# Host-laid inputs and a split first slab, and a last norm finished with tokens on partitions

## What is computed

```python
def rms_norm(x, gain):
    xf = x.astype(jnp.float32)
    y = xf * lax.rsqrt(jnp.mean(xf * xf, axis=-1, keepdims=True) + NORM_EPS)
    return (y * gain.astype(jnp.float32)).astype(x.dtype)
...
h = rms_norm(x, norm_mix[i])
q, kc, vc, ks, vs, kw, vw, gt = jnp.split(h @ w_in, splits, axis=-1)
```

## Time and profile before

| | us |
|---|---|
| median of 3 runs | 1273.48 |
| lowest, highest | 1270.31, 1273.67 |
| profiled execution | 1273.24 |
| its span in the trace | 1271.4 |
| TensorE busy (matmuls) | 1195.2 (94%) |
| DVE, ACT, POOL busy | 765.0, 565.6, 452.6 |

### The profile page before, as it was taken

One profiled execution on the slowest core, in us unless ns is written; L12 is line 12 of the kernel. 1 busy time (PEld: TensorE's weight loads), 2 busy tenths in 40 slices (PEclk: granted clock), 3 DMA queues, 4 the chain that ended last, 5 costly groups with the idle time before them and its releaser, 6 DMA issues.

```text
span 1271.4 us, 23862 instructions
## 1 busy us (share of the span) xinstructions
PE 1195.2 (94%) x9313; PEld 1130.8 (89%) x9313; DVE 765.0 (60%) x1093; ACT 565.6 (44%) x788; POOL 452.6 (36%) x430
## 2 busy tenths in 40 slices
PE   6998999999999888999999999998988898999996
PEld 5987678999999875999999998988978896999996
DVE  5753564767655566676765464436755657777544
ACT  4232344554544444455454336644353444545432
POOL 4522232266630433166651211113431303666401
PEclk9998799999999989999999999998999999999998
DMA  6651001666645540466665453243341453667551
GB/s 200 205 192 41 9 26 34 200 176 188 188 160 183 164 134 2 120 178 187 177 197 182 149 173 127 69 129 104 101 133 34 148 165 87 191 174 196 180 169 50
DMA packets 224581, 175.49 MB, mean 138 GB/s; under 512 B 7796, under 2 KB 205788, under 8 KB 224380
## 3 DMA queue, kind: packets, MB, share of 16 engines
q1 hardware_dynamic: 219052, 168.33, 44.4%
q10 hardware_dynamic: 5424, 6.09, 1.4%
...
HBM read 173.39 MB, written 1.05 MB: 137 GB/s over the span
## 4 chain that ended last, share of the span: by engine, by line
PE 81%; DVE 8%; ACT 3%; issue 3%; POOL 3%; DMA 1%; SPq 0%; ACTq 0%; DVEq 0%; POOLq 0%
PE bank L574 22%; PE bank L580 22%; PE bank L575 21%; PE bank L840 2%; DVE w_l L1512 2%; ACT w_h L1157 2%; PE bank L608 2%; PE bank L614 1%; PE bank L704 1%; PE bank L1013 1%; PE bank L808 1%; POOL work L2261 1%; DVE work L1627 1%; PE bank L848 1%; PE bank L692 1%
## 5 line engine op out<-in xcount | busy, mean ns | idle before, releaser
L574 PE MATMUL bank<-xh,w_h 128*128 128x256 f32 (+2 forms) x1792 | 451.6, 289 | 5.5 <-DVE xl L1530 4.1
L575 PE MATMUL bank<-xl,w_h 128*128 128x256 f32 (+2 forms) x1792 | 443.0, 284 | 0.0
L574 PEld LDWEIGHTS bank<-xh,w_h 128*128 128x128 f32 x1792 | 339.9, 190 | 8.5 <-issue 5.1
L575 PEld LDWEIGHTS bank<-xl,w_h 128*128 128x128 f32 x1792 | 340.8, 190 | 1.0
L1512 DVE TENSOR_TENSOR w_l<-raw,w_h 128x2048 fp32r<-128x2048 f32 (+3 forms) x95 | 212.2, 2234 | 158.6 <-ACT w_h L1157 158.5
L1157 ACT ACTIVATE w_h<-raw 128x2048 fp32r<-128x2048 f32 (+3 forms) x95 | 173.3, 1825 | 241.7 <-PE bank L580 220.5
L580 PE MATMUL bank<-xh,w_l 128*128 128x256 f32 (+2 forms) x1792 | 251.4, 283 | 2.9 <-DVE w_l L1512 2.9
L580 PEld LDWEIGHTS bank<-xh,w_l 128*128 128x128 f32 x1792 | 230.5, 189 | 3.3 <-DVE w_l L1512 3.1
L2183 POOL TENSOR_TENSOR work<-work 128x256 f32<-128x256 f32 x66 | 162.9, 2469 | 140.4 <-ACT work L1300 140.4
L1795 DVE TENSOR_TENSOR w_l<-raw,w_h 128x2048 fp32r<-128x2048 f32 x66 | 151.4, 2293 | 14.0 <-ACT w_h L1296 13.8
L574 PE MATMUL bank<-hid_h,w_h 128*128 128x256 f32 (+1 forms) x592 | 148.0, 284 | 2.5 <-issue 1.8
...
## 6 DMA issues: line engine op xcount, KB each, us to landing
...
raw<-in_w_in SPq DMA_DIRECT2D x26, 1024.0 KB, 5.2
...
raw<-in_nsa_w_in SPq DMA_DIRECT2D x10, 1024.0 KB, 5.4
...
raw<-in_swa_w_qkv SPq DMA_DIRECT2D x5, 1024.0 KB, 5.3
```

The costliest lines, as they stand in the source:

```text
L574: mm(dst, parts[0][:, k, cols], high, start=first, stop=False)
L575: mm(dst, parts[0][:, k, cols], low, start=False, stop=False)
```

## The change

**The host** lays out `x` with features on partitions (`xt_c`), the gains and biases as one table (`gain_c`), the convolution taps, position table and meta tokens likewise (`packed`). **The opening:** SP loads `x` in four parts and slab 0 in two halves, in the order part, half, part, part, half, part; the constants move behind slab 1 on the same queue, and three packed loads replace the 23. The transposes of `x` and of the small vectors are gone. `first_opening` computes chunks 0 and 1 together, half a slab at a time. ACT and DVE split slab 0 by halves. The table of roots is loaded first on ACT; `ones` is filled by POOL. **The end:** TensorE turns `h2` to tokens-on-partitions before the last FFN (`h_turn`, copied by ACT's `take_h` to `h_tok`). DVE's take of a last chunk also multiplies by the gain, ACT squares straight from the bank; `token_squares` sums them per token, with tokens on partitions, into two columns; `y_turn` turns the scaled chunks; then the root and reciprocal are of [128, 2], and the output is `bank * rstd + h_tok` in four pieces, three by DVE and one by ACT and POOL, with an output DMA for each.

```diff

     gains = [A["norm_mix"][0], A["norm_ffn"][0], A["norm_mix"][1], A["norm_ffn"][1], A["norm_final"],
...
+    xt = np.asarray(A["x"])[0].T.reshape(KC, 128, T1).transpose(1, 0, 2).reshape(128, KC * T1)
+    meta = np.asarray(A["meta_tokens_2"]).T.reshape(KC, 128, META).transpose(1, 0, 2)
+    return {"xt_c": xt, "gain_c": tab[:, 0], "taps_c": tab[:, 1:4], "pe_c": np.concatenate([pe, pe], 0), "meta_c": meta}


...
+        h_tok = work[:, stage + 3 * GN * T2:stage + 3 * GN * T2 + 2048].rearrange("p (b n) -> p b n", b=2)
+        o_sb = big[:, 0:2048].rearrange("p (b n) -> p b n", b=2)
+        y_part = big[:, 2048:2560]
+        tok_root, tok_rstd = meta_rstd[:, 0:2], meta_rstd[:, 2:4]
...
+        PIECES = [(0, 0, (y_taken, 1)), (1, 0, (y_stored, 2)), (0, 1, (y_taken, 2)), (1, 1, (y_taken, 3))]
+        Y_BANK = {(0, 0): 0, (1, 0): 1, (0, 1): 2, (1, 1): 4}
+        H_BANK = {(0, 0): 4, (1, 0): 5, (0, 1): 6, (1, 1): 3}
...
-            for tb in range(2):
-                sp.dma_start(x_in[:, tb, :], A["x"][0][128 * tb:128 * tb + 128, :]).then_inc(x_loaded, 16)
-            issue(0)
+            def x_part(j):
+                sp.dma_start(xT[:, 2 * j:2 * j + 2, 0:T1], A["xt_c"][:, 512 * j:512 * j + 512]
+                             .rearrange("p (c t) -> p c t", c=2)).then_inc(x_loaded[j], 16)
+
+            (whole, source), = slabs[0]
+            for half in range(2):
+                ks = slice(4 * half, 4 * half + 4)
+                x_part(2 * half)
+                sp.dma_start(whole[:, ks, :], source[:, ks, :]).then_inc(first_loaded[half], 16)
+                x_part(2 * half + 1)
             issue(1)
-            sp.wait_ge(prepared, 1)
-            for dst, src in vec_loads:
-                sp.dma_start(dst, src).then_inc(vec_loaded, 16)
+            sp.dma_start(early[:, :], A["early_c"]).then_inc(early_loaded, 16)
+            sp.dma_start(h2[:, :, 0:META], A["meta_c"]).then_inc(vec_loaded, 16)
+            sp.dma_start(pe_dup, A["pe_c"]).then_inc(vec_loaded, 16)
+            sp.dma_start(vecs[:, 1:4, :], A["taps_c"]).then_inc(vec_loaded, 16)
...
+            for k, (tb, half, by) in enumerate(PIECES):
+                sp.wait_ge(*by)
+                cols = slice(512 * half, 512 * half + 512)
+                sp.dma_start(out[0][128 * tb:128 * tb + 128, cols], o_sb[:, tb, cols]).then_inc(out_stored, 16)
...
-            pe.wait_ge(early_loaded, 16)
-            pe.wait_ge(x_loaded, 32)
-            for b in range(4):
-                turn([(bank[b][:, 256 * c + 128 * tb:256 * c + 128 * tb + 128],
-                          x_in[:, tb, 128 * (2 * b + c):128 * (2 * b + c) + 128]) for c in range(2) for tb in range(2)],
-                     turn_done)
-            pe.wait_ge(gain_loaded, 16)
-            turn([(bank[4][:, 0:KC], vec_in[0:KC, 0, :])], turn_done)
-
-            def turn_small():
-
-                pe.wait_ge(vec_loaded, 16 * len(vec_loads))
-                turn([(bank[5][:, 128 * v:128 * v + 128], vec_in[:, v, :]) for v in range(4)], turn_done)
...
+            def first_opening():
+
+                parts = view(w_h, 0, KC, 256), view(w_l, 0, KC, 256)
+                for half in range(2):
+                    ks = range(4 * half, 4 * half + 4)
+                    if half:
+                        pe.wait_ge(w_hi, 1)
+                    else:
+                        pe.wait_ge(first_hi, 1)
+                    for k in ks:
+                        pe.wait_ge(xl_ready, k + 1)
+                        for c in range(2):
+                            high_terms(bank[c][:, 0:T1], parts, k, slice(128 * c, 128 * c + 128), xh[:, k, 0:T1], xl[:, k, 0:T1],
+                                       k == 0)
+                    if half:
+                        pe.wait_ge(w_lo, 1)
+                    else:
+                        pe.wait_ge(first_lo, 1)
+                    for c in range(2):
+                        last = low_terms(bank[c][:, 0:T1], parts, [(k, k) for k in ks], slice(128 * c, 128 * c + 128),
+                                         xh[:, :, 0:T1], half == 1)
+                        if half:
+                            last.then_inc(proj_done, 1)
+                line["n"] += 2
...
+            first_opening()
+            pe.wait_ge(prepared, 1)
+            sum_squares(0, T1, 0, 8)
+            pe.wait_ge(early_loaded, 16)
+            m = 1
+            for n in range(2, 21):
                 if n <= 12 and n % 2 == 0 or n > 12 and n % 2:
...
+                if n in (2, 3):
+                    permute((proj_taken, n - 1))
...
+            def token_squares(c0, c1):
+
+                for c in range(c0, c1):
+                    pe.wait_ge(sq_ready, SQ_AT[8] + c + 1)
+                    for tb in range(2):
+                        last = mm(bank[7][:, tb:tb + 1], sq[:, c % 4, 128 * tb:128 * tb + 128], ones[:, 0:1], start=c == 0 and tb == 0, stop=c == 7,
+                                  skip_group_check=True)
+                    last.then_inc(ss_step, 1)
+
+            def y_turn(half):
+
+                for tb in range(2):
+                    turn([(bank[Y_BANK[tb, half]][:, 128 * c:128 * c + 128], xT[:, 4 * half + c, 128 * tb:128 * tb + 128])
+                          for c in range(4)], y_turned)
+
+            def h_turn(c):
+
+                for tb in range(2):
+                    last = nc.tensor.transpose(bank[H_BANK[tb, c // 4]][:, 128 * (c % 4):128 * (c % 4) + 128],
+                                               h2[:, c, META + 128 * tb:META + 128 * tb + 128], ident)
+                    if c % 4 == 3:
+                        last.then_inc(h_turned, 1)
+
...
+                if l == 2:
+                    pe.wait_ge(h_tok_ready, 4)
...
+                            if part == 0 and g and c == 3 and l == 2:
+                                pe.wait_ge(sq_ready, SQ_AT[8] + 4)
...
-                            sum_squares(norm, T, 0, 4)
+                            token_squares(0, 4)
+                            y_turn(0)
...
-                    sum_squares(norm, T, 4, 8)
+                    token_squares(4, 8)
+                    y_turn(1)
...
-            sum_squares(7, T2, 0, 8, LEAD)
+            for c in range(8):
+                sum_squares(7, T2, c, c + 1, LEAD)
+                if c == 4:
+                    pe.wait_ge(proj_taken, N_FFN[2])
+                h_turn(c)
...
-            act.dma_start(early[:, :], A["early_c"]).then_inc(early_loaded, 16)
+            act.dma_start(vecs[:, 0, :], A["gain_c"]).then_inc(gain_loaded, 16)
             act.wait_ge(prepared, 1)
-            act.dma_start(*gain_load).then_inc(gain_loaded, 16)
-            high(0)
+            fn(scrap[:, :], eps_col[:, 0:1], ACT.Sqrt)
...
+            act.wait_ge(gain_loaded, 16)
+            for half in range(2):
+                at = slice(1024 * half, 1024 * half + 1024)
+                for c in (4 * half + 1, 4 * half + 3):
+                    act.wait_ge(x_loaded[c // 2], 16)
+                    line.put(fn(xh[:, c, 0:T1], xT[:, c, 0:T1], ACT.Copy, scale=vec("g", c)), xh_odd)
+                    if c % 4 == 1:
+                        act.wait_ge(first_loaded[half], 16)
+                        fn(w_h[:, 0, at], raw[:, 0, at], ACT.Copy).then_inc(w_hi if half else first_hi, 1)
+            squares(0, T1, xT, lambda c: (x_loaded[c // 2], 16), lambda c: high(1) if c == 3 else None)
...
+            def down_last():
+
+                l, m = 2, ffn_at[2][1] + FC
+                for x in range(2, 8):
+                    high(m + x)
+                for c in range(8):
+                    if c == 4:
+                        preload_root()
+                    act.wait_ge(proj_taken, N_FFN[l] + 44 + c + 1)
+                    if c >= 4:
+                        act.wait_ge(ss_step, SS_AT[8] + c - 3)
+                    line.put(fn(sq[:, c % 4, 0:T1], bank[bank_of(N_FFN[l] + 44 + c)][:, 0:T1], ACT.Square), sq_ready)
+                    if c == 3:
+                        for x in range(8, 12):
+                            high(m + x)
+                act.wait_ge(ss_step, SS_AT[8] + 8)
+                line.put(fn(tok_root, bank[7][:, 0:2], ACT.Sqrt, bias=eps_col[:, 0:1]), root_ready)
+                tb, half, _ = PIECES[1]
+                act.wait_ge(y_scaled, 1)
+                act.wait_ge(y_turned, 1 + tb + 2 * half)
+                line.put(fn(y_part, bank[Y_BANK[tb, half]][:, :], ACT.Copy, scale=tok_rstd[:, tb:tb + 1]), y_stored)
+
+            def take_h():
+
+                for k, (tb, half) in enumerate(((0, 0), (1, 0), (0, 1), (1, 1))):
+                    act.wait_ge(h_turned, k + 1)
+                    line.put(fn(h_tok[:, tb, 512 * half:512 * half + 512], bank[H_BANK[tb, half]][:, :], ACT.Copy), h_tok_ready)
...
+            def first_low(half):
+
+                at = slice(1024 * half, 1024 * half + 1024)
+                if half:
+                    dve.wait_ge(w_hi, 1)
+                else:
+                    dve.wait_ge(first_hi, 1)
```

(41 more changed lines are left out.)

152 lines of the change are left out of this document (44 added, 108 removed).

## The result

The changed kernel took 1251.7 us, the median of four runs from 1249.96 to 1253.73, against 1271.89 for four runs of the kernel before beside it: a ratio of 0.9846, 95% interval 0.9813 to 0.9880, which is 1.5% less time. Its profiled execution took 1250.05 us (span 1248.3), the one before 1273.24 (span 1271.4). The forecast was 1255.0 with a range of 1250 to 1262. Later, with more runs, the change had a median of 1253.55 (six runs) against 1272.36 (eleven).

What follows compares the result with a forecast made beforehand. TensorE was taken to bound the kernel, with 81% of the chain, work being worth removing only where it waits. The terms -10.3 + 0.3 + 0.5 - 8.7 = -18.2 from the median 1273.48 gave 1255.0 us, range 1250 to 1262.

Steps and rivals of the forecast that it cites:

- Opening, 10.3: Start of kernel: chunk 2 starts at 18.2 instead of 28.58, gaining 10.3 us; bounds 7.9 and about 11.3.
- paced by ACT: Opening's sums of squares: squares 5 to 8 wait for four slots, so the old 3.62 us was kept.
- Is it kept: Chunk 4: opening's gain survives, slab 2's w_h and w_l ready with margins of 1.0 and 0.5 us.
- Entry of the last FFN, cost 0.3: Before the last FFN's first up matmul: 16 added transposes of h2 cost 0.3 us, from -0.9 to 0.7.
- wins at most 0.9: Last FFN's first 16 matmuls: 2.74 us, 1.9 at full pace, so a clock staying up wins at most 0.9.
- Down projection, cost 0.5: Last FFN's down projection: eight added transposes 0.94, sums 1.1 instead of 1.54; cost 0.5 us, bounds 0.4 and 1.3.
- The end, 8.7: After the last square: shorter root, reciprocal and output chain, span ending 1262.7 against 1271.4; gain 8.7 us, bounds 7.3 and 9.3.
- the late clock: Rival, opening: clock rises only at the old 20.0, gain there 7.9, total 1257.4 us; chance 0.12.
- POOL holds SP's queue: Rival, end: POOL's addition delays SP's queue and two pieces behind it; gain there 7.3, total 1256.4 us; chance 0.07.
- The supply: Rival, chunk 4: late tables make TensorE wait, one us per us past 22; more likely 1258 us; chance 0.10.
- the slower case: Rival, first projections: TensorE stays at 1.2 GHz, each us costing 0.5; 0.3% slower at 44 us; chance 0.01.

Runs made afterwards that it cites:

- opening_two: The change with ACT making xh of blocks 4 to 7, sums 0 to 3 earlier, all squares before slab 1's split: 1254.89 us, ratio 0.9836 to before.
- tables_late: The change with the three packed tables issued behind slabs 2 and 3: chunk 4 starts 9.03 us behind chunk 2 instead of 7.01.
- fill_alone: New opening with the old end, plus 16 unused identity transposes between the last FFN's sums of squares: first up matmul to low terms 2.0 us.
- change_repeat: The changed kernel itself, run again unaltered: median 1253.55 us of six runs; its profiled execution took 1262.25.
- both_bounds: The change with VectorE making w_l earlier, 15 extra matmuls before the first, POOL's output piece issued last: 1251.06 us, ratio 0.9833 to before.

## Why the prediction was right

*Opening, 10.3: right, 10.2 at chunk 4 and 10.0 from 60 us on, with luck in it.* First matmul 6.8, measured 6.95; end of the opening 14.6, measured 14.56; chunk 2 at 18.2, measured 17.83. Three sub-steps were off. The second half slab landed at 9.50, not 8.4; the low clock still hid it. The sums of squares took 3.27 us, not 3.62: that row counts the last one's tail, and they are not "paced by ACT" but 16 passes on TensorE, 0.20 each on average, and opening_two shows them as long with the squares ready. And 0.57 us of the 10.75 at chunk 2 is given back by chunk 4, as the ropes stand behind it; the prediction had the shift pass through. The last two cancel, so the sum was partly right for a wrong reason, and the wrong reason misled my next experiment.

*Is it kept: right.* The tables landed at 15.6 (15.5 forecast), by another two errors that cancel: the constants landed at 14.74, not 13.5, and the tables came 0.9 behind them, not 2. Slab 2's `w_h` was ready 1.6 us ahead of chunk 4 and its `w_l` 0.9 ahead of the low terms, where 1.0 and 0.5 had been priced. tables_late shows that this cover runs out as the rival said.

*Entry of the last FFN, cost 0.3: wrong sign, gain 0.74.* The transposes fell where the prediction put them: seven pairs behind ACT's squares, the eighth ahead of the first `up` matmul. The step that failed is the clock, "wins at most 0.9", which was taken as a bound and put at nothing in the sum. It gives back 0.74 in the 16 `up` matmuls, and in the last sum of squares it pays for the eighth pair. fill_alone shows that it is the transposes between the sums that do it, whatever they turn.

*Down projection, cost 0.5: inside the bounds, and nearer than it deserved.* The lead falls by 0.88 at the sums and turns (14.88 to 14.00), and in this pair of traces 0.31 comes back chunk by chunk, because the kernel before runs the rest of the half in 24.72 us, where all thirteen later profiles, with the old end or the new, take 24.41. From the last low term ahead of the sums to the last of all it is 28.08 us in every profile with the new down projection and 27.19 in the two later ones with the old: the cost is 0.89. The sums and turns in the change:

```profile
1212.00 1.84 PE L920 MATMUL bank<-ones,sq 128*128 128x1 f32 x16
1213.70 1.07 PE L621 MATMUL bank<-early,xT 128*128 128x128 f32 x8
1214.53 0.36 PE L587 MATMUL bank<-hid_h,w_h 128*128 128x256 f32 x1
```

The term that was sized too small is the sums: the one-column passes start 0.112 apart, as their weight loads do, 1.70 us for the sixteen and not 1.1, so the row of 128 columns was the nearer, not the 16-column one. The turns took 0.83 (0.94). What slowed the kernel before there is open.

*The end, 8.7: right, 8.8.* Root 0.26, reciprocal 0.17, DVE's pieces 0.69 (0.72), ACT's 0.69 (0.60), POOL 1.26 (1.6). SP's last issue starts 4.2 us behind the last square (4.1 forecast) and ends at 1245.8. SP's longest issue took 0.46 (0.34), the slowest landing 2.5 (2.8).

*Sum:* forecast 18.2; by parts, with 10.0 and 0.9 for the two terms above, 10.0 + 0.8 - 0.9 + 8.8 = 18.7; 20.2 and 18.8 by the two sets of medians. The time of 1255.0 was 3.3 too high in the first comparison, 2.0 of it in the gain, and 1.3 because the kernel before took 1271.89 there and not 1273.24.

*Rivals:* the late clock did happen, in part. In the executions with no extra matmuls the fast pace began 3.6 to 6.1 us after the first projection matmul (at 11.11 in the change, 12.42 in tables_late, 13.44 in change_repeat), and the opening took 10.8 to 11.7 us, in nearly the same order: up to 0.8 us for chunk 2, not 2.4. The change and change_repeat are one kernel and lie 1.9 us apart in this delay (4.2 and 6.1), so it is chance of the execution and not only of the code. POOL holds SP's queue for 0.6, by both_bounds. The supply and the slower case did not come. Against the slower case the prediction said that no later slice of the clock is below eight tenths; one stands at seven, and the 19 us beside it belong to seven tenths.
